# The decay's low-rank product made one head group earlier, behind the third score level

## The reference

```python
proj = h @ w_in_l
(gq, gk, gv, gg, glr, hq, hf, hi, hg, ga, gb) = jnp.split(proj, split_points, axis=-1)
log_a = jax.nn.log_sigmoid((glr @ w_lr2_l + b_lr_l).astype(jnp.float32)) / GLA_TAU
...
b = jnp.cumsum(gc, axis=2)
scores = jnp.einsum('bhtk,bhsk,bhtsk->bhts', qc, kc, decay)
```

## Time and profile before

| | us |
|---|---|
| median of 3 runs | 1048.87 (1048.65 to 1049.21) |
| the profiled execution | 1049.85 |
| its span, first to last instruction | 1048.0 |
| PE busy | 1033.6 (99%) |
| DVE busy | 685.7 (65%) |
| ACT busy | 491.2 (47%) |
| granted TensorE clock, mean | 0.999 |

### The profile page before, as it was taken

How to read it: one execution, slowest core, us unless ns; L and a number is a source line. 1 busy time by engine, 2 the same in 40 slices (tenths; PEclk the granted TensorE clock), 3 DMA queues, 4 the chain that set the end, 5 groups by cost and what they waited for, 6 DMA issues and landing times.

```text
span 1048.0 us, 23454 instructions
## 1 busy us (share of the span) xinstructions
PE 1033.6 (99%) x10156; PEld 956.7 (91%) x10156; DVE 685.7 (65%) x1034; ACT 491.2 (47%) x771; POOL 66.7 (6%) x86
## 2 busy tenths in 40 slices
PE   7999999999999999999999999999999999999997
PEld 6988999989999899999899878999999999888886
DVE  6266645676626757456756578988888888744544
ACT  6433454722736344546327557644444444633532
POOL 5200002100004000031000000000000000000000
PEclk9999999999999999999999999999999999999999
DMA  7522223622317232345222281142342332422212
GB/s 196 161 82 66 78 72 102 193 71 70 83 49 215 83 82 62 83 120 172 69 75 89 80 299 38 42 121 81 90 112 81 98 105 61 141 81 81 84 57 90
DMA packets 130774, 105.20 MB, mean 100 GB/s; under 512 B 4272, under 2 KB 115888, under 8 KB 130672
## 3 DMA queue, kind: packets, MB, share of 16 engines
q1 hardware_dynamic: 125808, 85.88, 28.6%
q0 software_dynamic: 4864, 17.83, 5.7%
HBM read 91.89 MB, written 11.80 MB: 99 GB/s over the span
## 4 chain that ended last, share of the span: by engine, by line
PE 92%; DVE 4%; ACT 1%; DVEq 1%; DMA 1%; issue 0%; ACTq 0%
PE ps L290 35%; PE ps L1945 21%; PE ps L1969 13%; PE ps L1212 10%; PE ps L405 3%; PE ps L1145 2%; PE ps L1120 1%; PE ps L1135 1%; PE ps L1147 1%; PE ps L1152 1%; PE ps L1104 1%; PE ps L1184 1%; DVE h_t L972 1%; PE ps L1116 1%; PE ps L1172 0%; PE ps L1086 0%
## 5 line engine op out<-in xcount | busy, mean ns | idle before, releaser
L276 ACT ACTIVATE w_hi_t<-w_raw_t 128x1024 fp32r<-128x1024 f32 x73 | 77.2, 1057 | 261.3 <-PE ps L290 179.0
L290 PE MATMUL ps<-x_hi,w_lo_t 128*128 128x288 f32 x896 | 195.6, 300 | 0.0
L290 PE MATMUL ps<-x_hi,w_hi_t 128*128 128x288 f32 x896 | 191.7, 296 | 0.0
L290 PE MATMUL ps<-x_lo,w_hi_t 128*128 128x288 f32 x896 | 191.2, 295 | 0.0
L280 DVE TENSOR_TENSOR w_lo_t<-w_raw_t,w_hi_t 128x1024 fp32r<-128x1024 f32 x73 | 89.4, 1225 | 136.4 <-ACT w_hi_t L276 135.3
L290 PEld LDWEIGHTS ps<-x_hi,w_lo_t 128*128 128x128 f32 x896 | 143.3, 188 | 4.4 <-issue 2.5
L290 PEld LDWEIGHTS ps<-x_lo,w_hi_t 128*128 128x128 f32 x896 | 144.0, 188 | 0.0
L290 PEld LDWEIGHTS ps<-x_hi,w_hi_t 128*128 128x128 f32 x896 | 144.0, 188 | 0.0
L1945 PE MATMUL ps<-x_hi,w_lo_t 128*128 128x288 f32 x276 | 81.4, 295 | 0.6 <-issue 0.6
L1945 PE MATMUL ps<-x_lo,w_hi_t 128*128 128x288 f32 x276 | 81.4, 295 | 0.0
L1945 PE MATMUL ps<-x_hi,w_hi_t 128*128 128x288 f32 x276 | 81.3, 295 | 0.0
(11 more groups left out here) (347 smaller groups left out, 2281.3 us busy)
## 6 DMA issues: line engine op xcount, KB each, us to landing
w_raw_t<-in_w_in_dram SPq DMA_DIRECT2D x57, 512.0 KB, 3.8
merged<-in_w_ffn_in_dram SPq DMA_DIRECT2D x22, 512.0 KB, 5.2
w_raw_t<-in_w_ffn_in_dram SPq DMA_DIRECT2D x22, 512.0 KB, 4.6
w_raw_t<-in_w_ffn_out_dram SPq DMA_DIRECT2D x22, 512.0 KB, 3.7
w_raw_t<-in_w_in_dram SPq DMA_DIRECT2D x32, 256.0 KB, 3.8
h_t<-in_x_prompt_dram SPq DMA_DIRECT2D x8, 512.0 KB, 5.6
h_t<-in_state_gla_dram POOLq DMA_DIRECT2D x4, 1024.0 KB, 6.0
h_t<-in_state_hgrn_dram POOLq DMA_DIRECT2D x8, 512.0 KB, 7.6
```

Of the source, the lines that this page charges most:

```text
L276: nc.scalar.activation(w_hi_t[:, u % NSPL, 0:nk, :], w_raw_t[:, u % NRAW, 0:nk, :], ACT.Copy).then_inc(w_hi, 1)
L290: m = nc.tensor.matmul(out[:, q, :], w[:, u % NSPL, k, :], x(k, q), start=first and i == 0, stop=last and i == len(todo) - 1)
```

## The change

The product of group 0 stays where it was. The product of group j + 1 (j = 0, 1, 2) is made in slot 9 of group j (`DECAY_NEXT`), behind level2, and no longer in slot 2 of its own group. ACT copies it out in slot 10 of group j; the rest of the decay's work on ACT stays in slot 3. No operation is added or taken away. Since the order of the slots also numbers the uses of the places, the product's use of place 0 now comes right behind the values' use and ahead of level3's, where it used to come behind ss2 and ahead of norm2.

```diff
-NOW = {2: ["decay"], 6: ["level0"], 8: ["level1"], 9: ["level2"],
+NOW = {6: ["level0"], 8: ["level1"], 9: ["level2"],
...
+DECAY_NEXT = 9
 def slot_steps(j, n):
     names = [(j, s) for s in NOW.get(n, [])] + [(j - 1, s) for s in (LATE if j < G else LAST).get(n, [])]
+    if (j, n) == (0, 2):
+        names.append((0, "decay"))
+    if n == DECAY_NEXT:
+        names.append((j + 1, "decay"))
     return [(h, s) for h, s in names if 0 <= h < G]
...
-        def decays(j):
+        def decay_in(j):
 
             s = step(j, "decay")
             freed(act.activation(halves(Z[:, 0, :]), s.rearrange("p (a b) -> p a b", a=2)[:, :, 0:HT],
                                  ACT.Identity, bias=blr4[:, j:j + 1]), j, "decay")
+
+        def decays(j):
+
             act.drain()
             act.activation(T3[:, :, :], Z[:, :, :], ACT.Abs)
...
                 if n == 3:
+                    if j == 0:
+                        decay_in(0)
                     decays(j)
...
+                if n == DECAY_NEXT + 1:
+                    if j + 1 < G:
+                        decay_in(j + 1)
                 if n == 10:
                     act.preload_act_table_set("sigmoid_and_others")
```

## The result

The changed kernel takes 1066.73 us in the median (1066.56 to 1067.49) against 1048.98 for the kernel before: a ratio of 1.017, 95% interval 1.0159 to 1.018. It is 17.8 us slower. Forecast were 11.2 us slower, 1060.1 us with a range of 1058.0 to 1064.5: right in direction, in place and in the wait, and outside the range in size.

The account below looks back on a forecast made before the run. PE was taken to bound the kernel: +13.9 us for three late products in slot 9, -2.6 us given back in slot 2, +11.2 us in sum, so 1060.1 us, range 1058.0 to 1064.5.

Parts of the forecast that it names:

- What bounds the kernel: PE, busy 99% of the span, sets the time; every microsecond it gains or loses reaches the end.
- What slot 2 gives back: Taking the product out of slot 2 in groups 1 to 3 saves 0.88 us each, 2.6 us in all.
- The release in slot 9: The product waits for DVE's addition to free place 0; next unit 4.62 us late, three times, 13.9 us.
- What waits behind it: All later PE work is delayed, nothing absorbs it; level3 doesn't wait for ACT's 0.74 us copy of the product.
- The array tiling: One tiling mode change less per group, worth at most 0.1 to 0.2 us each; left out of the sum.
- the first rival: PE's clock also falls at the three gaps; three falls add 4.1 to 6.9 us: 1064 to 1067; chance 0.15.
- The price: Cost of one clock fall, taken from slow transposes at the program's start: 1.4 us, or 2.3 at half speed.
- The second and third rival: Slot 9: no wait, 1048.3 us, chance 0.05; or DVE's chain faster or gap partly made up, 1057.7 us, chance 0.05.

Follow-up runs that it names:

- e2: The changed kernel with 14 matmuls of ones ahead of each waiting product, to fill the gap: 1060.83 us.
- e1: The changed kernel with the values' place given back earlier: ACT's swap ahead of its slot 10 splitting, DVE's addition ahead of level3's multiplications: 1048.42 us.
- e4: The changed kernel with the product made behind level4 in slot 11, not behind level2 in slot 9: 1048.87 us.
- e5: The changed kernel with DVE's addition that gives the values' place back moved ahead of one weight splitting, gaps 2.72 us: 1060.78 us.
- e3: The changed kernel with only group 1's product moved, into slot 9 of group 0; groups 2 and 3 keep it in slot 2: 1055.62 us.
- e6: The changed kernel with 7 matmuls of ones at the start of each gap, leaving 2.10 us idle: 1064.06 us.

## Why the prediction was right in kind and wrong in size

**What bounds the kernel**: right. PE's delays reached the end in full; the lag grew gap by gap and nothing made it up.

**What slot 2 gives back**: 0.88 us forecast for each group, 0.87 read from the lag in slot 2 of group 3.

**The release in slot 9**: right. The wait names DVE's addition, and 3.86 us of idle time and 0.06 us of handing over are the forecast's chain. With the clock held up (e2) the time was 1060.83 for 1060.1.

**What waits behind it**: right. Level3 had no wait for ACT's copy.

**The array tiling**: e1 and e4 both have one change of mode less in a group, and their times are not to be told from the kernel before. Their traces can be. Against the trace before, e1 loses 0.69 us at the product in slot 9 of group 0 and gains 0.87 us in slot 2 of group 1, where the product was; e4 gives the same two numbers, the loss in its slot 11. The difference of 0.2 us a group is within the prediction's 0.1 to 0.2, but it wasn't left out of the sum: 0.69 us charged and 0.88 given back have it in already. That it comes from the mode and not from something else at slot 2 is argued, not shown.

**The step that failed** is the first rival, in the sentence "A gap of 3.9 us is just shorter", and with it the chance of 0.15 and the range. I had one fall in the trace, at the end of the program, and took its 4.4 us after the last work as the idle time that it takes. The runs show no such fixed time: the clock fell 2.0, 4.1 and 3.5 us after the last matmul at the three gaps of the changed kernel, the second time with PE at work again, and in e5 each time with PE at work again. The end of the program shows it too. In e4 PE's last matmul ends at 1041.78 and the clock falls at 1044.0, 2.2 us later (PE in order of time, then stretches as above):

```profile
1041.15 0.63 PE L1982 MATMUL ps<-w_hi,x_lo 128*128 128x512 f32 x2
```

```profile
1043.00:1044.00 1.00, 0.00 (x0) 0.00 (x0) 0.94 (x2) 0.16 (x1) 0.00 (x0) 0.98 0.58 219
1044.00:1045.00 1.00, 0.00 (x0) 0.00 (x0) 0.75 (x1) 0.00 (x0) 0.00 (x0) 0.50 0.19 74
```

Over the eight traces this time at the end goes from 2.0 us (e3) to 4.8 us (e1), so one reading of 4.4 us could not carry the sentence. Three falls should have been the main case. The price was right in sum and rough for one fall: 1.4 to 2.3 us from the slow stretch at the start, against 2.2, 1.5 and 2.9 us, 6.6 in all where the first rival had 4.1 to 6.9. The dear falls are those with the longer low stretches (6.8 us against 3.4 us). My range, up to 1064.5, took in only the lowest end of three falls by my own price (1064 to 1067), and the measured 1066.73 lies in that span.

The Trainium skill's rule stood against the change and was the better guide. It stands in TensorE: Matmul & The Clock Gate, Why this matters for your kernels (the prediction named a section that the page doesn't have). It advises against idle gaps between bursts; the three gaps of 3.86 us agree, and those of 2.72 and 2.10 us in e5 and e6 show that somewhat shorter ones are not safe either.

**The second and third rival**: no trace of either. The gaps were 3.85 to 3.86 us in all three groups.

**Still open**: what decides whether and when the clock falls at a gap of a given length. The cause of the 0.5 us stop in group 2 of the changed kernel is open too, but it doesn't need the gaps: e4, which has none, has a stop of 0.4 us at the same matmul, 0.24 us of it put down to issue.

## What to carry to other kernels

When a step moves in a fixed order and its buffer is handed on by count, look up who holds that buffer at the new place and when it is given back; here an operation of 0.7 us, which had found its place free in slot 2, waited in slot 9 for an addition that stands fourth among DVE's instructions behind level2. When PE is the bound, a gap can cost twice, as here: its length, and a stretch at half clock at its end or behind it, which at gaps of 2.7 to 3.9 us came in all seven cases traced and was worth 1.5 to 2.9 us. To tell the two parts from one another, fill the gap with matmuls that nobody needs, as in e2; to get rid of both, give the buffer back earlier or step to a slot where it is free, as in e1 and e4.

## What the runs showed of the hardware that wasn't expected

The low clock came in pieces of two lengths: 3.4 us (group 1 of the changed kernel, all three of e5) and 6.8 us (groups 0 and 2 of the changed kernel, e3, e6). Falls came from 2.0 to 4.8 us after the last work, also up to 1.7 us after PE had taken up its work again, so a gap and the slow matmuls that belong to it can be apart in a trace. At the lower clock a pair of 288-column matmuls took 0.48 us against 0.266, 1.8 times and not twice.

The start of the program has the same kind of spread: PE's 24 transposes took 4.62 us before and 3.52 us in the changed kernel's trace, between the same neighbours. This is the clock as well, though the column of the granted clock shows 1.00 there in both. The record of the clock in the trace before begins only at 12.75 us, and at that moment the transposes, until then 0.21 us apart, become 0.11 us apart. In the changed kernel the record begins at 8.33 us, ahead of the first transpose, and but for two waits nearly all are 0.11 us apart from the start. The other six traces agree: the pace changes where the record begins, at 8.4 or at 12.6 to 13.2 us. So a 1.00 ahead of the first entry says nothing, and the slow stretch from which the prediction took its price was itself a mixture, 17 transposes at the slow pace and 7 at the fast one. The kernel before took 1048.18 to 1050.13 us over the 21 executions beside e1 to e4; how much of that comes from the start isn't shown.
